# Two 16-expert layers: from bins of one expert group (96 places, four experts each) to bins of one expert (64 places), with a 17th bin and other weight loads

## What is computed

```python
N_EXPERTS_2 = 16
N_GROUPS = 4
GROUP_SIZE = N_EXPERTS_2 // N_GROUPS
D_EXPERT = D_MODEL // 2
...
    scores = jax.nn.sigmoid(jnp.dot(xt.astype(jnp.float32), router_w.astype(jnp.float32)))
    sel = scores + router_b.astype(jnp.float32)
    group_score = lax.top_k(sel.reshape(-1, N_GROUPS, GROUP_SIZE), TOP_K)[0].sum(-1)
    top_group = jnp.argmax(group_score, axis=-1)
    expert_group = jnp.arange(N_EXPERTS_2) // GROUP_SIZE
    in_group = expert_group[None, :] == top_group[:, None]
    _, idx = lax.top_k(jnp.where(in_group, sel, -jnp.inf), TOP_K)
...
    for e in range(N_EXPERTS_2):
        h = jax.nn.silu(xt @ w_gate[e]) * (xt @ w_up[e])
        out = out + combine[:, e:e + 1] * (h @ w_down[e])
```

## Time and profile before

| | us |
|---|---|
| median of 3 runs (2549.83 to 2553.07) | 2550.6 |
| the profiled execution's own time | 2545.95 |
| its span, first to last instruction | 2544.2 |
| gather to last scatter of `MOEA` | 1783.65 to 2085.49: 301.8 |
| gather to last scatter of `MOEB` | 2228.32 to 2529.62: 301.3 |

### The profile page before, as it was taken

How to read it: one execution, slowest core, us unless ns; L and a number is a source line. 1 busy time by engine, 2 the same in 40 slices (tenths; PEclk the granted TensorE clock), 3 DMA queues, 4 the chain that set the end, 5 groups by cost and what they waited for, 6 DMA issues and landing times. The chain is left out here.

```text
span 2544.2 us, 34498 instructions
## 1 busy us (share of the span) xinstructions
PE 2360.1 (93%) x15206; PEld 1002.0 (39%) x15206; DVE 487.6 (19%) x1168; ACT 366.0 (14%) x868; POOL 33.0 (1%) x78
## 2 busy tenths in 40 slices
PE   4999989998999899999999999886999989799997
PEld 1574634443865332222223222253422227342222
DVE  2143830002094300000000000213100021310002
ACT  2023420001232210000000000121100011110000
POOL 2000000000000000000000000000000000000000
PEclk9999989999999999999999999997999999899999
DMA  8231286444354799999999999812899972479993
GB/s 292 77 122 66 100 286 228 152 141 176 117 207 166 265 316 351 366 364 367 364 366 366 363 364 367 287 64 99 293 364 364 359 274 76 129 244 364 365 359 145
DMA packets 446103, 644.55 MB, mean 253 GB/s; under 512 B 10723, under 2 KB 345019, under 8 KB 445947
## 3 DMA queue, kind: packets, MB, share of 16 engines
q1 hardware_dynamic: 442011, 629.55, 72.0%
q0 software_dynamic: 3936, 12.69, 1.5%
HBM read 641.15 MB, written 1.05 MB: 252 GB/s over the span
## 5 line engine op out<-in xcount | busy, mean ns | idle before, releaser
L1080 PE MATMUL bank<-ring,wide 128*32 128x512 f32 x7296 | 808.2, 595 | 1.7 <-ACT wide L1663 0.9
L1080 PEld LDWEIGHTS bank<-ring,wide 128*32 128x32 f32 x7296 | 231.8, 110 | 548.6 <-issue 548.5
L1108 PE MATMUL bank<-dreg,RB 128*32 128x512 f32 x3648 | 415.0, 595 | 0.0
L1670 ACT ACTIVATE SG<-bank 128x256 f32<-128x256 f32 x114 | 43.7, 383 | 1187.2 <-PE bank L1080 1187.2
L1108 PEld LDWEIGHTS bank<-dreg,RB 128*32 128x32 f32 x3648 | 106.8, 109 | 223.8 <-issue 223.8
L719 PE MATMUL bank<-wide,ring 128*128 128x256 f32 x832 | 182.1, 381 | 0.0
L719 PEld LDWEIGHTS bank<-wide,ring 128*128 128x128 f32 x832 | 158.9, 191 | 23.0 <-issue 1.4
L2409 DVE TENSOR_TENSOR H<-SG,bank 128x256 f32<-128x256 f32 x66 | 27.8, 421 | 717.3 <-ACT SG L1670 717.3
L1007 PE MATMUL bank<-ring,wide 128*128 128x512 f32 x352 | 156.2, 597 | 4.4 <-DVE MODX L1997 4.4
L709 PE MATMUL bank<-ring,wide 128*128 128x512 f32 x352 | 155.2, 599 | 1.0 <-DMA ring<-in_w_kv 1.0
L709 PE MATMUL bank<-ring,T 128*128 128x512 f32 x256 | 113.4, 603 | 1.4 <-ACT sm L1842 0.8
(11 more groups left out here) (388 smaller groups left out, 1403.0 us busy)
## 6 DMA issues: line engine op xcount, KB each, us to landing
ring<-in_l_moe_w SPq DMA_DIRECT2D x176, 1024.0 KB, 11.5
dreg<-in_l_moe_w SPq DMA_DIRECT2D x88, 1024.0 KB, 12.4
ring<-in_w_gate SPq DMA_DIRECT2D x64, 1024.0 KB, 11.3
ring<-in_w_up SPq DMA_DIRECT2D x64, 1024.0 KB, 13.5
dreg<-in_w_down SPq DMA_DIRECT2D x64, 1024.0 KB, 12.2
ring<-in_l_mod_w SPq DMA_DIRECT2D x24, 2048.0 KB, 8.0
ring<-in_l_ffn_w SPq DMA_DIRECT2D x22, 1024.0 KB, 10.1
ring<-in_l_w_in SPq DMA_DIRECT2D x7, 2048.0 KB, 9.0
```

The costliest lines, as they stand in the source:

```text
L1080: mm = pe.matmul(banks[r % 2][32 * g:32 * g + 32, :], xg[:, k, at:at + 32], ring[:, i % RING, k, :], start=k == 0, stop=k == KC - 1)
L1108: return pe.matmul(banks[4 + 2 * (b % 2) + h][32 * g:32 * g + 32, :], HQ[:, r % 4, j, 32 * q:32 * q + 32], dring[:, i % RING, j, h * NCH:( ...
L1670: act.activation(SG[:, r % 2, :], banks[r % 2][:, 0:FSTEP], ACT.Silu).then_inc(sem("moe_silued"), 1)
```

## The change

`MOE1` keeps its 8 bins of 96 places. `MOEA` and `MOEB` get one bin for each expert with 64 places (2 chunks), and a 17th bin which takes the places over 64 of the fullest expert. That is 34 blocks in 17 rounds; round r is bin r. The 17th bin loads the fullest expert's three matrices once more, at an address that SP works out from a number it reads from `flag`. Two bins share one pass of places, results and scatters ("unit", 9 in all); gates are multiplied in with the places. The gathers are cut into quarters of four bins (4 matmuls with 256 columns a call): four calls ahead of round 0, one in each of the rounds 0 to 11, and the 17th bin's (64 columns, 16 matmuls) in round 13. Scatters come two a round from round 4 on.

The ring is read as pairs of blocks: a pair is loaded in a low and a high half of the 1024 input rows, each half a slot, and a slot is free when the low or high half of `up` is through. In `MOE1` the pieces are rows of 512 numbers (256 where a pair lies over two experts). In `MOEA` and `MOEB` a partition gets 8 neighbouring input rows, so that one half is 2048 numbers in one piece; the gather then takes every 8th column of the tokens as its weight operand.

```diff
     def __init__(self, name, experts, steps, chunks):
...
+        self.cap = 32 * chunks
+        self.bins = experts + (chunks == 2)
+        self.blocks = self.bins * steps
+        self.rounds = self.blocks * chunks // 4
+        self.units = self.bins if chunks == 3 else (self.bins + 1) // 2
+        self.pairs = self.blocks // 2
...
-MOE1 = Moe("1", NE1, 1, NSTEP)
-MOEA = Moe("A", NG, GS, NSTEP2)
+MOE1 = Moe("1", NE1, NSTEP, 3)
+MOEA = Moe("A", NE2, NSTEP2, 2)
...
+                    if not fullest:
+                        i = MOES.index(m)
+                        sp.wait_ge(sem("fullest"), i)
+                        fullest.append(sp.value_load(flag[0:1, 3 + i:4 + i], min_val=0, max_val=m.experts - 1))
+                    return fullest[0]
...
+                def up(q):
+                    for h, passed in enumerate(("upped_low", "upped")):
+                        slot = 2 * (q % 2) + h
+                        if q < 2:
+                            slot_free(slot)
+                        else:
+                            sp.wait_ge(sem(f"moe_{passed}"), m.before[passed] + m.done_in(2 * (q - 2) + 1) + 1)
+                        for i, w in enumerate((w1, w3)):
+                            for e, lo, n, at in m.runs(q):
+                                rows = w(expert(e)).rearrange("(k p) n -> p k n" if m is MOE1 else "(p k) n -> p k n", p=P)
+                                sp.dma_start(pairs[:, slot, i, :, at:at + n], rows[:, 4 * h:4 * h + 4, lo:lo + n]).then_inc(
...
+                    for q in range(2, m.pairs):
+                        up(q)
+                        if q >= 4:
+                            down(2 * q - 4)
+                            down(2 * q - 3)
...
-                def slot_gates():
...
+                def gather_quarter(n, o):
...
+                            i = pe.matmul(o[:, j * w:(j + 1) * w], src[:, t, :].rearrange("p (d k) -> p k d", k=KC)[:, k, :],
+                                          PMQ[q % 2][:, t, 0:w], start=t == 0, stop=t == 1)
...
+                        if r < 12 or r == 13:
+                            if left:
+                                upto(*left)
+                            gather_quarter(gathered, banks[3])
...
+                        for i in m.ended(r - 2):
+                            down(i)
+                            if r >= 4 and r <= m.rounds:
+                                scatter_pair(scattered // 4, scattered % 4, banks[3], left)
...
+                        if (r % 2 == 1 and r >= 3) or r == m.rounds + 1:
+                            turn_places(turned, ("added", scattered) if r == m.rounds + 1 else left)
```

More of the change, by code:

```diff
@@ new lines, in counts, with runs @@
+        n |= {"all_placed": TT if self.chunks == 3 else 5 * TT, "down_done": self.blocks}
+        n |= {f"up_in{p}": self.loaded(self.pairs - 1 - (self.pairs - 1 - p) % 2) for p in range(2)}
+        n |= {f"down_in{s}": 16 * len(range(s, self.blocks, RING)) for s in range(RING)}
+        return n
+    def runs(self, q):
+        cols = lambda i: (i // self.steps, i % self.steps * FSTEP)
+        (a, lo), (b, lo2) = cols(2 * q), cols(2 * q + 1)
+        return [(a, lo, 2 * FSTEP, 0)] if a == b else [(a, lo, FSTEP, 0), (b, lo2, FSTEP, FSTEP)]
@@ L392, in unrolled @@
         def unrolled(m):
-            return 1 if m is MOE1 else m.halves
+            return 1 if m is MOE1 else m.steps
         def baton_bin(m):
@@ L1075, in up @@
+                def up(r):
+                    if m is MOE1 and r in (0, m.starts(4)):
+                        upto("gather_taken", 2 * KC if r else KC)
+                    if m is not MOE1 and r % 4 == 0:
+                        upto("gather_taken", r + 4 if r < 16 else 17)
                     if r >= 2:
                         upto("hidden", r - 1)
-                    for k in range(KC):
-                        for g, (i, c) in enumerate(m.pieces(r)):
-                            at = CAP * (i // m.steps) + 32 * c
-                            mm = pe.matmul(banks[r % 2][32 * g:32 * g + 32, :], xg[:, k, at:at + 32], ring[:, i % RING, k, :],
-                                           start=k == 0, stop=k == KC - 1)
@@ L1165, in moe, with scatter_pair @@
-                for p in range(4):
-                    scatter(final, p, banks[p])
+                def scatter_pair(u, p, o, free):
+                    t, h = divmod(p, 2)
+                    rows = slice(0, P) if 2 * u + 1 < m.bins else slice(64 * h, 64 * h + 64)
+                    upto("places_taken", u + 1)
+                    upto("ys_ready", u + 1)
+                    upto(*free)
+                    pe.matmul(o[:, :], PTMs[u % 2][rows, 2 * h + t, :], YS[rows, h * NCH:(h + 1) * NCH], start=True, stop=True).then_inc(
+                        sem("moe_scattered"), 1)
@@ new lines, in triple_rounds @@
+                def triple_rounds():
+                    for n in range(KC):
+                        gather(n)
+                    final = m.bins - 1
+                    for r in range(m.rounds + 3):
+                        if r < m.rounds:
+                            up(r)
+                        if 1 <= r <= m.rounds:
+                            turn_hidden(r - 1)
+                        if r == m.last_down(final):
+                            turn_places(final)
+                        for i in m.ended(r - 2):
+                            down(i)
+                        if r < KC:
+                            gather(KC + r)
+                        for b in range(final):
+                            if r == m.last_down(b):
+                                turn_places(b)
+                            p = r - m.last_down(b) - 2
+                            if 0 <= p < 4:
+                                scatter(b, p, banks[3])
+                    for p in range(4):
+                        scatter(final, p, banks[p])
@@ L2438, in moe @@
                         multiply(r)
+                    if m is not MOE1:
+                        if 4 <= r <= m.rounds:
+                            for p in range(2):
+                                add(r // 2 - 2, 2 * (r % 2) + p, banks[3])
+                        if r == m.rounds + 1:
+                            for p in range(4):
+                                add(final - 1, p, banks[p])
+                        if r >= 2 and r % 2 == 0 and r < m.rounds:
+                            place_slots(r // 2 - 1)
+                        if r == m.rounds:
+                            place_slots(final)
+                        if r in (3, 7, 11):
+                            one_hots(m, 2 + r // 4)
+                        continue
                     for b in range(m.bins):
```

365 lines of the change are left out of this document (216 added, 149 removed).

## The result

The changed kernel takes 2511.62 us in the median of 4 runs (2510.33 to 2512.28), the kernel before 2550.69 in 4 runs beside it (2549.83 to 2553.07). The ratio is 0.9845, with a 95% interval of 0.9828 to 0.9862: 39 us faster, where 50 were forecast. The changed kernel's profiled execution took 2512.16 us, its span is 2510.4.

What follows compares the result with a forecast made beforehand. PE was taken to set the time, with the loads nearly level. A layer's 10.1 + 241.7 + 22.8 plus 1 gave 275.6 us, 26 less than 301.5; 50 us for two layers gave 2500.6, own range 2486 to 2512.

Steps and rivals of the forecast that it cites:

- the rule that speaks against the change: Gather's weight operand in the later layers: SBUF lines are 16 bytes, a step of 8 float32 would pay; priced at nothing.
- rival 1: Later layers' gathers: strided weight loads bind; 12 us a layer at 1.5 times, gain gone at 1.9; chances 0.10 and 0.13.
- The 17th bin's gather: Round 13: 32 rows of 64 columns at the weight load's 0.191 us each, 6.1 us, making the round 20.6.
- The start: First four gather calls of a later layer: 7.0 us, about 2 for the low clock, 0.9 for ACT's copy; 10.1 to round 0.
- fullest_bin: 16 small DVE operations behind the one-hot rows, beside PE's gather: cost nothing, or 3 us once if a gather waited.
- 0.110 a row: PE's unit price for `down`, from 5.29 us / 48; two blocks of 16 rows a round were 3.53 us.
- some tenths a round: Possible cost of more operand-width changes between short groups in the later layers; 52 us for two layers was taken as 50.
- The waits at bank 3: Odd rounds: `turn_places` waits 0.87 us for DVE's addition; the rival of waits before each scatter had chance 0.10.
- The end: Round 17 without `up`, then last scatters, `down`, `turn_places` and two waits of 1.9 us for ACT: 22.8 us a layer.
- What PE needed before: Rounds of the earlier kernel: 11.1 us of PE work on average against 11.4 us of loads, within 3%.
- the test of prices: Unit prices applied to the earlier layer gave 300 us against 301.8 and 301.3; 1 us was added to the new sum.
- Rival 2: Later layers: loads become the bound; 2520 if 2048-number pieces ran at 348 GB/s, no change if all did; chances 0.07 and 0.02.

Runs made afterwards that it cites:

- rows256: Changed kernel with the gather reading neighbouring columns and the later layers' gate and up loads in pieces of 256 numbers: 2535.51 us, ratio 0.9939.
- rows512: Changed kernel with the gather reading neighbouring columns and the later layers' loads in pieces of 512 numbers instead of 2048: 2498.67 us, ratio 0.9794.
- gcopy: Changed kernel with ScalarE copying the tokens into column order once a layer, so the gather reads neighbours; loads stay at 2048 numbers: 2493.69 us, ratio 0.9770.
- best_512: rows512 with the quarter gather between the halves of `up`, scatters ahead of `down`, and expert counts copied ahead of the one-hot rows: 2496.20 us, ratio 0.9786.

## Why the prediction was right, and where it was off

The direction, the place and the mechanism were as forecast: PE sets the time before and after, the gain is in the two later layers alone, `MOE1` is unchanged. Of the 26 us a layer forecast, 19 to 20 came. No run undoes the bins alone; `rows256` and `rows512` keep them, read neighbours in the gather, and are 15 and 52 us faster than the kernel before. The time lies 0.4 us inside the upper end of the forecast's own range (2486 to 2512), and that is in part luck: strides priced at nothing cost 9 to 10 us a layer, and two other terms were counted 2.8 and 2.5 us a layer too high. With those two right the forecast would have been some 2490, and its own range would not have held the time. Term by term, `MOEA`:

| term | forecast | after | `gcopy` |
|---|---|---|---|
| gather to round 0 | 10.1 | 11.24 | 10.86 |
| rounds 0 to 3 | 43.7 | 45.0 | 43.8 |
| rounds 4 to 11 | 123.8 | 127.7 | 125.4 |
| round 12 | 13.0 | 13.2 | 13.2 |
| round 13, with the 17th bin's gather | 20.6 | 23.4 | 18.2 |
| rounds 14 to 16 | 40.5 | 41.0 | 41.0 |
| end | 22.8 | 20.0 | 20.0 |
| sum | 274.6 | 281.5 | 272.5 |

**The step that failed** is the one on the rule that speaks against the change: "The low bound is no cost", and "I take no cost". The weight loads took 335 ns, 1.75 times, and the argument against it (each number already has over 1.4 ns) was wrong. The prediction's sign for rival 1, gather rows over 0.22 us with weight loads over 0.2, came true. So did the rival, in part: its price was too high, as it took each row to last as long as its load. A call of 8 rows took 2.12 us, 0.265 a row, where `gcopy`'s took 1.82; within a call, loads of 335 ns start 0.24 us apart, so they overlap in part. `gcopy` gives the whole price: 281.5 - 272.5 = 9.0 us in `MOEA`, of which 5.1 is round 13, 3.5 the twelve calls and 0.4 the start; and 10.4 in `MOEB`, of which 6.6 is round 13. By rival 1's formula, 335 ns would have been 14.8 + 4.6 = 19.4 a layer.

**The 17th bin's gather** was mis-sized both ways. The price "0.191 each", a load after the other, gave 6.1 us; without the step it took 3.62, 0.113 a row, as loads of 190 ns overlap each other. With the step it took 7.71, 0.241 a row, and the lower clock cost the matmuls behind it another 1.0 (`MOEA`) and 2.5 (`MOEB`).

**The start** missed by 1.1: the gather took 10.55 us instead of some 9, and 10.18 in `gcopy`, so that 0.4 is the strides and most of the rest the clock: it was at 0.50 for some 6 us of the gather, where it had been for 4 before the change. `fullest_bin` was priced at nothing "or 3 us once if a gather waited for them"; a gather does wait, 1.07 us longer in each later layer. I had looked at who produces the gather's operand, and not at who last reads the bank that it writes.

**`down`** cost 1.85 us for 16 rows where I counted 1.77: `0.110 a row` was read from groups of 48, and a switch of operands adds about 0.1 us a group. That is the "some tenths a round" of the sum, 0.1 to 0.2 once the gather is cheap (14.92 against 14.75). **`turn_hidden`** was 0.27 ahead of a gather instead of 0.37. **The waits at bank 3** were right: 0.88 in odd rounds only, 12.3 us in 14 waits over both layers.

**The end** was 2.8 us shorter than counted. The waits for ACT were counted at 1.9 each, and the one ahead of unit 7's scatters was 0.69. The last unit is one bin of 64 places, so its scatters have 64 rows, taken from the upper and the lower half of the rows in turn; in the trace such a pair overlaps in time, 0.12 us apart. All 8 took 2.08 us and not the 3.67 of the earlier trace rows.

**What PE needed before** was taken too low. From round 5 of `MOEA` on, a round took 11.6 us on average and not 11.1, so PE was above the loads' 11.4 and not below, as SP's waits in the earlier trace rows say too. And most of the 1.8 us that the test of prices missed is in the earlier trace rows: the first 128 `up` matmuls took 15.64 us and not 14.0, as the granted clock was 0.52 over their first 3 us, behind the small matmuls of `slot_gates`. That went with `slot_gates`, so the 1 us "of the test" should not have been added.

**The loads** were sized well: 417 GB/s against 410, no wait. Rival 2 did not come with 2048-number pieces; with pieces of 256 it does, and `rows256` shows it.

The rule of the Trainium skill (SBUF — State Buffer, section Door 1: The DMA port swizzle) said what I set aside. It says two things that differ for float32. That a 16-byte line has to be hit twice or more for the full rate agrees with the runs: 2 numbers a line, 206 ns; one a line or one in two lines, 329 and 335. That float32 may step by 4 for free does not: a step of 4 took 329 ns. The measurements decide, for weight loads.

## What to carry to other kernels

Before changing the layout that a load leaves in SBUF, look at how TensorE's weight operand walks over it. A step of 2 float32 cost next to nothing here, one of 4 or 8 took the load from some 200 to 330 ns; one pass that puts the operand in order, on an engine that is idle then, paid for itself (18 us for two operations in each of two layers).

Before adding readers to a bank, ask which matmul writes it next. And price a size of transfer by the bytes of a stage over its rate, as a first estimate: 106.9 MB at 367, 393 and 417 GB/s gave 291, 272 and 256 us, and the two kernels that waited for loads took 290 to 294 and 272. A faster load is worth what PE waits for it, which was nothing in `MOE1`, under 1 us a layer in `rows512` and 5 in `best_512`.

## What the runs showed of the hardware

- A float32 weight load of 128 columns: 201 to 203 ns (neighbours), 206 (every 2nd), 329 (every 4th), 335 (every 8th), as means with the parts at a lower clock in them; medians 190, 196, 330 and 337. At a granted clock of 0.50 a load of neighbours takes up to 337 too, and one of every 8th number takes no longer than at 1.00.
- Weight loads overlap each other in the trace: 32 of 190 ns in 3.68 us with 64-column matmuls, and 32 of 335 ns in 7.78.
- A gather of 64 columns with loads of 335 ns had the granted clock fall from 1.00 to 0.50 on the way, in eight layers of eight, though PE was never idle; the same with loads of 190 or 196 ns kept 1.00.
- Eight 512-column matmuls of 64 rows, from the upper and the lower half in turn, took 2.08 us at full clock, and eight of 128 rows 3.67.
- Loads by piece, one core in these layers: 367 GB/s at 256 numbers for `up` with 1024 for `down`, 393 at 512, 409 at 1024, 417 at 2048.
